# Differential attention with queries on partitions, norm per partition, fp32 scores, and no GpSimd in the heads

## What is computed

```python
def diff_attention(h, w_q, lam_vecs, subln_g, w_o, k, v, slopes, lam_init):
    ...
        s = jnp.einsum('bqhcd,bkhcd->bhcqk', qb, k).astype(jnp.float32) * scale
        p = jax.nn.softmax(s + bias[None, :, None], axis=-1)
        w = p[:, :, 0] - lam * p[:, :, 1]
        return jnp.einsum('bhqk,bkhe->bqhe', w.astype(v.dtype), v)
    ...
    o = rmsnorm(o, subln_g, SUBLN_EPS) * (1.0 - lam_init)
    return o.reshape(B, S, V_WIDTH) @ w_o
```

## Time and profile before

| what | value |
|---|---|
| median of 3 runs | 1179.99 us |
| lowest and highest | 1178.47 and 1181.94 us |
| span of the profiled execution | 1174.9 us |
| PE busy | 1108.2 us, 94% of the span |
| PE weight loads busy | 887.3 us, 76% |
| DVE busy | 653.9 us, 56% |
| ACT busy | 480.1 us, 41% |
| POOL busy | 202.2 us, 17% |

### The profile page before, as it was taken

How to read it: one execution, slowest core, us unless ns; L and a number is a source line. 1 busy time by engine, 2 the same in 40 slices (tenths; PEclk the granted TensorE clock), 3 DMA queues, 4 the chain that set the end, 5 groups by cost and what they waited for, 6 DMA issues and landing times.

```text
span 1174.9 us, 13923 instructions
## 1 busy us (share of the span) xinstructions
PE 1108.2 (94%) x4856; PEld 887.3 (76%) x4856; DVE 653.9 (56%) x937; ACT 480.1 (41%) x745; POOL 202.2 (17%) x141
## 2 busy tenths in 40 slices
PE   8889689999999999999998989889999999999995
PEld 5667568888888888888876656668888888888884
DVE  7997985543443433446467787867533433433434
ACT  6448554422322422434335655745422422422342
POOL 4556733000000000012012242223000000000013
PEclk9989899999999999999999999999999999999998
DMA  5112213222223222232311111113222232222322
GB/s 221 54 54 72 81 48 122 90 90 97 101 90 107 89 97 99 89 108 90 108 54 55 54 53 37 36 54 126 90 98 100 90 107 89 95 102 89 107 72 72
DMA packets 30293, 102.42 MB, mean 87 GB/s; under 512 B 3248, under 2 KB 5552, under 8 KB 30128
## 3 DMA queue, kind: packets, MB, share of 16 engines
q1 hardware_dynamic: 29968, 100.74, 24.9%
q10 hardware_dynamic: 288, 1.18, 0.3%
HBM read 99.81 MB, written 2.10 MB: 87 GB/s over the span
## 4 chain that ended last, share of the span: by engine, by line
PE 78%; DVE 15%; ACT 4%; issue 2%; POOL 1%; DMA 0%; DVEq 0%; SPq 0%; ACTq 0%
PE ps L1251 70%; PE ps L1369 4%; DVE gelu L923 2%; DVE prob L1142 1%; ACT prob L705 1%; PE ps L1432 1%; DVE w_lo L822 1%; DVE lru_v L923 1%; DVE prob L1139 1%; DVE lru_v L949 1%; PE ps L1406 1%; DVE lru_r L985 1%; DVE inv_lam L1137 1%; DVE h_lo L827 1%; DVE lru_v L989 1%
## 5 line engine op out<-in xcount | busy, mean ns | idle before, releaser
L1251 PE MATMUL ps<-u_hi,w_hi 128*128 128x512 f32 x696 | 281.7, 405 | 16.9 <-POOL u_lo L409 12.0
L486 ACT ACTIVATE w_hi<-w_raw 128x1024 fp32r<-128x1024 f32 x184 | 193.5, 1052 | 245.8 <-PE ps L1251 196.8
L1251 PE MATMUL ps<-h_hi,w_hi 128*128 128x512 f32 x704 | 282.5, 401 | 3.5 <-DVE h_lo L827 2.2
L1251 PE MATMUL ps<-h_lo,w_hi 128*128 128x512 f32 x704 | 277.8, 395 | 0.0
L1251 PE MATMUL ps<-h_hi,w_lo 128*128 128x512 f32 x704 | 277.8, 395 | 0.0
L1251 PE MATMUL ps<-u_lo,w_hi 128*128 128x512 f32 x696 | 272.8, 392 | 0.0
L1251 PE MATMUL ps<-u_hi,w_lo 128*128 128x512 f32 x696 | 272.8, 392 | 0.0
L822 DVE TENSOR_TENSOR w_lo<-w_raw,w_hi 128x1024 fp32r<-128x1024 f32 x164 | 204.4, 1247 | 17.7 <-ACT w_hi L486 17.6
L1251 PEld LDWEIGHTS ps<-u_hi,w_hi 128*128 128x128 f32 x696 | 131.4, 189 | 52.8 <-issue 11.3
L1251 PEld LDWEIGHTS ps<-h_hi,w_hi 128*128 128x128 f32 x704 | 134.6, 191 | 35.6 <-DVE h_lo L827 4.1
L1251 PEld LDWEIGHTS ps<-h_lo,w_hi 128*128 128x128 f32 x704 | 134.7, 191 | 28.6 <-issue 1.0
(11 more groups left out here) (174 smaller groups left out, 1010.2 us busy)
## 6 DMA issues: line engine op xcount, KB each, us to landing
w_raw<-weights SPq DMA_DIRECT2D x184, 512.0 KB, 3.2
x<-x_t SPq DMA_DIRECT2D x8, 256.0 KB, 5.4
y_t<-att SPq DMA_DIRECT2D x8, 256.0 KB, 2.3
gelu<-gate_weights ACTq DMA_DIRECT2D x1, 1024.0 KB, 5.7
lam_in<-lam_vecs ACTq DMA_DIRECT2D x1, 128.0 KB, 2.0
vec<-vectors SPq DMA_DIRECT2D x1, 64.5 KB, 1.9
```

The lines of the kernel that those rows point to most:

```text
L486: nc.scalar.activation(w_hi[:, t % RING, :], w_raw[:, t % RAWS, :], ACT.Copy).then_inc(whi_done, 1)
L1251: ins = nc.tensor.matmul(ps[:, bank, :], w[:, slot, ws], o[:, k, :], start=(k == 0 and n == 0), stop=(k == NCH - 1 and n == 2))
```

## The change

Attention is written anew; all else stays.

- The result has queries on partitions: `attend(h, j)` is done for each j, with the transposed probabilities of 128 queries as stationary operand and 128 columns of `value` as moving operand (ten 128x128 products a head), and `prob_t` holds two blocks of queries rather than a head. `value_h` is gone.
- Scores are one pair of fp32 matmuls for every j. kq_hi, kq_lo and the four instructions a head that make them are gone. `kq` has two buffers.
- `combined` doesn't divide: it adds the second exponentials, times minus lambda times the ratio of the sums, to the first. The norm afterwards makes the factor irrelevant, if its epsilon is scaled with the square of the first sum, which `variance` does.
- The norm is per partition: ACT squares four 128x128 blocks of bank O with a sum along each (`squares`), then works on 128x4 numbers (`sub_guess_of`), DVE too (`variance`, `sub_newton`), and ACT copies the four blocks out with a scale per partition (`scaled`).
- `back(h)` on PE transposes the four blocks of the scaled result into bank T; ACT makes att_hi from it (`attended_hi`) and DVE att_lo (`attended_lo`), which are the operands of the output projection.
- POOL does nothing in the heads: DVE makes all w_lo of these tiles, and the Newton step.
- The heads are written out, not looped. Steps of head h-1 (its last transposition and attend, the norm, back) stand within head h.
- New waits: `attend(h, 0)` for o_scaled of the head before (bank O is free), `transposes(h, 2)` for att_lo of the head before (bank T is free).

Added and unchanged lines of the new code, with the removed lines that matter:

```diff
+        late = ExitStack()
+        value = sb("value", [P, QB, D], F32, late)
+        late.close()
+        att_hi = sb("att_hi", [P, HEADS, S], F32R)
+        att_lo = sb("att_lo", [P, HEADS, S], F32R)
-        prob_t = sb("prob_t", [P, QB, S], F32)
-        kq = sb("kq", [P, 2, S], F32)
-        kq_hi = sb("kq_hi", [P, 2, S], F32R)
-        kq_lo = sb("kq_lo", [P, 2, S], F32R)
-        value_h = sb("value_h", [P, 2, QB, P], F32)
+        prob_t = sb("prob_t", [P, 2, S], F32)
+        kq = sb("kq", [P, 2, 2, S], F32)
-        sub = work[:, 0:3, :]
-        o_raw = work[:, 3, :]
+        o_rows = work[:, 0, :]
+        o_square = work[:, 1, :]
...
-            pool.wait_ge(bank_read, T_QK)
-            head_values(0, None, 0)
-            head_values(1, None, 1)
-            head_split_lo(0, None)
-            with pool.Fori(0, (HEADS - 2) // 2) as i:
-                own.enter(i, 4)
-                for k in range(2):
-                    head_values(2 + k, i, k)
-                    sub_newton(k, i)
-                    head_split_lo(1 + k, i)
-                own.leave((HEADS - 2) // 2)
-            head_split_lo(HEADS - 1, None)
-            sub_newton(HEADS - 2, None)
...
-                act.wait_ge(scores_read, at(2 * a + 2, i, 4 * QB))
+                    act.wait_ge(scores_read, 2 * a + c + 1)
...
+            def transposed(h, j):
                 a = QB * h + j
+                n = (QB - j) * P
+                act.wait_ge(trans_mm, a + 1)
+                if a >= 2:
+                    act.wait_ge(att_mm, a - 1)
+                nc.scalar.activation(prob_t[:, j % 2, 0:n], ps[:, BANK_T, 0:n],
+                                     ACT.Copy).then_inc(trans_read, 1)
+            def rows(j):
+                return slice((QB - 1 - j) * P, (QB - j) * P)
+            def squares(h):
+                act.wait_ge(att_mm, QB * (h + 1))
+                for j in range(QB):
+                    ins = nc.scalar.activation(o_square[:, rows(j)], ps[:, BANK_O, rows(j)], ACT.Square,
+                                               accum_out=o_stats[:, h % 2, 0, j:j + 1])
+                ins.then_inc(att_sq, 1)
+            def sub_guess_of(h):
+                act.wait_ge(var_done, h + 1)
+                own.step(nc.scalar.activation(o_stats[:, h % 2, 2, :], o_stats[:, h % 2, 1, :], ACT.Ln))
+                own.wait()
+                nc.scalar.activation(o_stats[:, h % 2, 2, :], o_stats[:, h % 2, 2, :], ACT.Exp,
+                                     scale=-0.5).then_inc(sub_guess, 1)
+            def scaled(h):
+                act.wait_ge(sub_rstd, h + 1)
+                if h:
+                    act.wait_ge(back_mm, h)
+                for j in range(QB):
+                    ins = nc.scalar.activation(o_rows[:, rows(j)], ps[:, BANK_O, rows(j)], ACT.Copy,
+                                               scale=o_stats[:, h % 2, 4, j:j + 1])
+                ins.then_inc(o_scaled, 1)
+            def attended_hi(h):
+                act.wait_ge(back_mm, h + 1)
+                nc.scalar.activation(att_hi[:, h, :], ps[:, BANK_T, :], ACT.Copy,
+                                     scale=lam_s[:, 6:7]).then_inc(ohi_done, 1)
...
+            for h in range(HEADS):
                 t = T_QK + 2 * h + RING
+                split_hi(t)
+                split_hi(t + 1)
+                if h:
+                    transposed(h - 1, 3)
+                exps(h, 0)
+                if h:
+                    squares(h - 1)
+                exps(h, 1)
+                if h:
+                    sub_guess_of(h - 1)
+                exps(h, 2)
+                transposed(h, 0)
+                if h:
+                    scaled(h - 1)
+                transposed(h, 1)
+                exps(h, 3)
+                if h:
+                    attended_hi(h - 1)
+                transposed(h, 2)
+            h = HEADS - 1
+            transposed(h, 3)
+            squares(h)
+            sub_guess_of(h)
+            scaled(h)
+            attended_hi(h)
...
-                own.step(nc.vector.tensor_scalar(prob[:, s, 1, 0:n], prob[:, s, 1, 0:n],
-                                                 inv_lam[:, s:s + 1], None, ALU.mult))
+                own.step(nc.vector.reciprocal(inv[:, s:s + 1], total[:, h % 2, j, 1:2]))
+                own.wait()
+                own.step(nc.vector.scalar_tensor_tensor(
+                    out=ratio[:, s:s + 1], in0=inv[:, s:s + 1], scalar=neg_lam,
+                    in1=total[:, h % 2, j, 0:1], op0=ALU.mult, op1=ALU.mult))
+                own.wait()
+                nc.vector.scalar_tensor_tensor(out=prob[:, s, 0, 0:n], in0=prob[:, s, 1, 0:n],
+                                               scalar=ratio[:, s:s + 1], in1=prob[:, s, 0, 0:n],
                                                op0=ALU.mult, op1=ALU.add).then_inc(prob_done, 1)
+            def variance(h):
+                first = total[:, h % 2, :, 0:1].rearrange("p q o -> p (q o)")
+                own.step(nc.vector.scalar_tensor_tensor(
+                    out=o_stats[:, h % 2, 3, :], in0=first, scalar=SUBLN_EPS, in1=first, op0=ALU.mult,
+                    op1=ALU.mult))
+                dve.wait_ge(att_sq, h + 1)
+                own.wait()
+                nc.vector.scalar_tensor_tensor(
+                    out=o_stats[:, h % 2, 1, :], in0=o_stats[:, h % 2, 0, :], scalar=1.0 / V_DIM,
+                    in1=o_stats[:, h % 2, 3, :], op0=ALU.mult, op1=ALU.add).then_inc(var_done, 1)
+            def sub_newton(h):
+                v, g, tmp = o_stats[:, h % 2, 1, :], o_stats[:, h % 2, 2, :], o_stats[:, h % 2, 3, :]
+                dve.wait_ge(sub_guess, h + 1)
+                own.step(nc.vector.tensor_tensor(tmp, g, g, ALU.mult))
+                own.wait()
+                own.step(nc.vector.scalar_tensor_tensor(out=tmp, in0=tmp, scalar=-0.5, in1=v,
+                                                        op0=ALU.mult, op1=ALU.mult))
+                own.wait()
+                nc.vector.scalar_tensor_tensor(out=o_stats[:, h % 2, 4, :], in0=tmp, scalar=1.5, in1=g,
+                                               op0=ALU.add, op1=ALU.mult).then_inc(sub_rstd, 1)
+            def attended_lo(h):
+                dve.wait_ge(ohi_done, O_ATT + h + 1)
+                nc.vector.scalar_tensor_tensor(out=att_lo[:, h, :], in0=ps[:, BANK_T, :],
+                                               scalar=sub_gain, in1=att_hi[:, h, :], op0=ALU.mult,
+                                               op1=ALU.subtract).then_inc(olo_done, 1)
...
+            for h in range(HEADS):
+                last = h == HEADS - 1
                 t = T_QK + 2 * h + RING
+                key(h)
+                split_lo(t)
+                biased(h, 0)
+                biased(h, 1)
+                combined(h, 0)
+                if h:
+                    variance(h - 1)
+                biased(h, 2)
+                combined(h, 1)
                 if not last:
+                    query(h + 1)
+                if h:
+                    sub_newton(h - 1)
+                biased(h, 3)
+                dve.wait_ge(scores_read, 2 * QB * (h + 1))
                 if not last:
+                    own.step(nc.vector.tensor_scalar(bias[:, :], bias[:, :], 0.5, None, ALU.mult))
+                split_lo(t + 1)
+                combined(h, 2)
+                combined(h, 3)
+                if h:
+                    attended_lo(h - 1)
+                own.wait()
+            h = HEADS - 1
+            variance(h)
+            sub_newton(h)
+            attended_lo(h)
...
-                products = ((kq_hi, kq_hi), (kq_hi, kq_lo), (kq_lo, kq_hi))
+                if a >= 2:
+                    pe.wait_ge(scores_read, 2 * (a - 1))
+                for c in range(2):
+                    rows = slice(c * HEAD_DIM, (c + 1) * HEAD_DIM)
+                    ins = nc.tensor.matmul(ps[:, BANK_SCORES + 2 * (j % 2) + c, 0:n],
+                                           kq[rows, h % 2, 1, qb * P:(qb + 1) * P],
+                                           kq[rows, h % 2, 0, 0:n], start=True, stop=True)
                 ins.then_inc(scores_mm, 1)
+            def transposes(h, j):
                 a = QB * h + j
+                pe.wait_ge(prob_done, a + 1)
+                if a >= 1:
+                    pe.wait_ge(trans_read, a)
+                if h and j == 2:
+                    pe.wait_ge(olo_done, O_ATT + h)
+                for kb in range(QB - j):
                     ks = slice(kb * P, (kb + 1) * P)
                     ins = nc.tensor.transpose(ps[:, BANK_T, ks], prob[:, j % 2, 0, ks], ident[:, :])
                 ins.then_inc(trans_mm, 1)
+            def attend(h, j):
+                a = QB * h + j
+                qb = QB - 1 - j
+                pe.wait_ge(trans_read, a + 1)
+                if h and j == 0:
+                    pe.wait_ge(o_scaled, h)
+                for kb in range(qb + 1):
```

(76 more changed lines are left out.)

288 lines of the change are left out of this document (37 added, 251 removed).

## The result

| | before | after |
|---|---|---|
| median | 1179.86 us (1178.46 to 1182.61) | 1182.58 us (1180.03 to 1184.33) |
| span of the profiled execution | 1174.9 us | 1180.7 us |
| granted clock, mean | 0.979 | 0.978 |

The ratio is 1.0023, with an interval of 1.0014 to 1.0031: the changed kernel is 2.7 us slower. The forecast was 1171.5 us, 8.5 faster, with a range from 1163 to 1181.

A forecast was written before the change was run, and what follows sets the result against it. PE was taken to wait about 2.8 us in each of six heads for a DVE instruction that POOL stretches. Six heads save 6.0, the first loses 0.65, the last stretch saves 3.2: 8.5 us, giving 1171.5 us, range 1163 to 1181.

The forecast's parts named there:

- The forecast has none or one: Attention heads: new PE waits of 1.9 us bring at most one fall to the lower clock level.
- in all seven: Rival: the clock falls in all seven heads, 1182.5 us; two or more falls had a chance of 0.22.
- Wait: 1.9: Before `attend(h, 0)`: PE waits 1.9 us for o_scaled of the head before, a 3.9 us chain against 2.0 of cover.
- Wait: 0.6: Before `transposes(h, 2)`: PE waits 0.6 us for att_lo of the head before, 4.45 us chain against 3.85 of cover.
- 18.6: PE's own work in a head after the change, in us, up 0.5 from 18.1 before.
- The sum itself: Whole attention: 6.0 us saved in six heads, 0.65 lost in the first, 3.2 saved in the last stretch: 8.5.
- the rival with serial scores: Score blocks: fp32 halves run one after the other, 2.1 us more a head, 15.4 in all, 1186.9 us; chance 0.10.
- "5.1 less than the median", "I take the offset as unchanged": Whole kernel: profiled span 1174.9 us lies 5.1 below the median 1179.99; same offset after, so span 1166.4.
- The 1157 us of a version without these waits: Attention heads: without both new waits a head takes 18.8 us, the whole 1157; shorter waits, 1157 to 1168, chance 0.15.
- GpSimd was not the cause: Rival: DVE's STT stays at 2.4 us without POOL beside it; nearly excluded by a 0.48 us row, no separate chance.

The follow-up runs named there:

- the kernel with the wait filled: Changed kernel with nine unused 128x512 matmuls per head on PE, ahead of `attend(h, 0)`, in the wait for bank O: 1177.69 us.
- the kernel with the query moved: Changed kernel with `query(h + 1)` behind `sub_newton` instead of ahead of it on DVE, nothing else: 1177.77 us.
- the kernels with the norm earlier: Changed kernel with `sub_newton` and `scaled` moved ahead: 1163.52 us; with two more steps moved, 1156.29; or with the second w_lo on POOL, 1159.22.
- its five variants: Changed kernel with norm steps earlier (1163.52 us), that plus two moves (1156.29), that plus POOL's second w_lo (1159.22), only query moved (1177.77), or wait filled (1177.69).

## Where the prediction went wrong

Both new waits and their causes were found. What failed is how many falls of the clock the waits bring, and the size of the wait for bank O. From the first key to the last passes of attention (603.12 to 791.33) the changed kernel takes 188.2 us where the one before took 183.9; the forecast was 8.5 less, so it missed by 12.8. One row of the kernel before bears on the first step below, the longest wait of its last stretch:

```profile
773.34 0.33 PE L1419 MATMUL ps<-ident,prob 128*128 128x128 f32 x1 [1.25 <-DVE prob L1142]
```

By its steps:

- **"The forecast has none or one"** fall of the clock. Wrong, five, and the largest part: four at 1.15 each, and a fifth in the last stretch at 1.5 (from the key of head 7 on it takes 33.7 us, against 32.3 in the kernel with the wait filled), 6.1 us in all. I put 1.9 on the safe side because waits of 2.67 to 2.86 were followed by a fall in three heads of six, and a stretch whose waits are "all shorter than 1.9" had none. That reading left out how much shorter: the longest wait there is the 1.25 us above, so nothing was known of waits between 1.25 and 2.67. The runs show that waits of 1.9 us are followed by a fall in four of eight (three of seven in the kernel with the query moved, and the one of this length in the changed kernel, at 771.77), and those of 2.5 us in four of six. The rival with a fall "in all seven", 1182.5, lies nearest to the result in time, but by luck: it has more falls and shorter waits than there were. In heads with a fall the second wait is shorter, 0.26 to 0.44 us where it is 0.77 in the others, since a slower PE meets it later. With the 0.3 to 0.5 us that this takes up, 1.15 comes to 1.5 to 1.7, about what a fall cost before (1.57).
- **"Wait: 1.9"** for bank O. Wrong, 2.51, and 1.91 where 1.3 was said for the last head: 7 x 0.61 = 4.3 us. PE's cover was right, 2.05 us from 743.92 to the start of the wait; the chain is 748.48 - 743.92 = 4.56 us where the forecast had 3.9. The link that was most mis-sized is the four copies on ACT: they start every 0.26 us and take 1.14, where I had overlapped the 0.28 of a plain copy down to 0.81 in all. With a scale per partition one takes 0.37. The next is the first link: from PE's next part at 743.92 to `biased(h, 2)` at 744.34 it is 0.42, not 0.20. The hand-over from ACT to PE is 0.14, not 0.04, and the two small operations of `combined` take 0.45, not 0.40. The other links came out as priced or a little shorter.
- **"Wait: 0.6"** for att_lo. Nearly right, 0.77, together 1.0 us in six heads.
- **PE's work, "18.6"**. 18.82, together 1.3 us in six heads, and 0.2 in the last stretch. The growth was nearly right: the row of a head before at full clock has 18.43, so it is 0.4 where 0.5 was forecast. The base was low: the pieces add up to 18.1 for that head, 0.3 under its own row, and the sum was not held against it. Of the pieces, the score blocks came out as worked out: 2.26 us for j = 0 and 1 with the transposition left out (2.33 forecast), 0.84 for j = 2 (0.85). The eight matmuls of `attend(h, 0)` take 0.97 us, not 0.86.
- **The sum itself.** Six heads at 22.07 - 21.1 save 5.8 us, not 6.0; the waits and the work named for the last stretch add up to 31.4, not 31.25. That is 0.3 us. (The 15.4 in the rival with serial scores should be 15.2 as well.) The first head takes 17.5 us where 17.66 was said.
- **"5.1 less than the median", "I take the offset as unchanged".** Wrong as a reading, though the forecast of the time doesn't use it, only that of the span. A run's time is 1.8 us above its own span after, and 2.6 before. The profiled execution of before was merely a quick one, some 2.5 us below the middle of the rest. Of the 5.8 us by which the two profiled spans differ, 1.4 also lie ahead of attention, in code that the change doesn't touch. Timed against each other the kernels differ by 2.7.

The sums, 6.1 + 4.3 + 1.0 + 1.5 + 0.3, less 0.2 for the first head, make 13.0 for the 12.8.

Right were: the cause in the kernel before (GpSimd beside the STT, 15 us by itself), that PE's work grows a little, that fp32 pairs overlap, and both places where PE would wait and whom it would wait for. The 1157 us of a version without these waits came out too, in part by luck. The rival with scores as the bound is refuted, and so is "GpSimd was not the cause".

So the gain did not stay away; it was given back. Taking GpSimd's subtraction away brings PE's waits for `prob` from 18.7 to 6.9 us and the falls from three to none, 15 us in time. The change takes away all 18.7, and puts 16.9 for bank O, 4.4 for att_lo and five falls in their place.

Not settled is which waits a fall follows. In the changed kernel the waits that end at 634.66 and 656.76 are both 2.51 us, and the clock falls after the second alone. I can give only how often it does, from one profiled execution of each kernel.

## What to carry to other kernels

When a change takes away a wait, walk the lists of the waiting engine's suppliers from the last release to the next one with measured durations, hand-overs included, and then ask of each link whether it must stand there: here moving two steps ahead made 1182.6 into 1163.5 us, and moving two more made 1156.3. Give the new wait a range in the forecast, since the chain here was 0.6 us longer than its links as I had priced them, out of a gain of 1.0 a head. Where a fall of the clock has been seen after some waits, the forecast has to price the new waits with it: here half of those of 1.9 us had one, and that belonged in the sum, not among the rivals.

## What the runs showed of the hardware

- Waits of PE and falls to the lower clock level in attention: up to 1.39 us, none (the kernels with the norm earlier, and the kernel before with its w_lo on DVE); 1.56 us, none (the last att_lo, in the changed kernel and its five variants); 1.9 us, four of eight; 2.5 us, four of six; 2.7 to 2.9 us, three of six. A fall costs 1.1 to 1.6 us, of which a later wait can take up a part. Filling the waits with matmuls that nobody needs removed all falls and won 4.9 us.
- An ACT copy of 128x128 from PSUM with a scale per partition takes 0.37 us, without one 0.28, and four in a row start 0.26 us apart.
- An operation of POOL that reads SBUF stretches DVE even at 128x1 (1.05 us against 0.16): DVE's ended at 654.00 and POOL's at 653.98. What such an instruction costs thus went by the end of POOL's here, not by its own size; that it does so in general is not shown.
- fp32 products of depth 64 on the two halves of the array's rows overlap at 512 and 384 columns as they do at 128. Beyond four cycles a column at 2.4 GHz, an estimate from attend's columns, the blocks of the changed kernel leave about 0.4 us each for entering and leaving. The tiling page of the Trainium skill ("Key Properties") says that a change of tiling mode drains the array. No run here shows what the 0.4 us consist of.
